# Input projections of a two-layer trunk: norm, turn, modulation and splitting tile by tile with the first panel's products

## The reference, cut to what matters

```
def rms_norm(x, g):
    y = xf * lax.rsqrt(jnp.mean(xf * xf, axis=-1, keepdims=True) + EPS)
    return (y * g.astype(jnp.float32)).astype(x.dtype)
def modulate(x, g, shift, scale):
    return rms_norm(x, g) * (1 + scale) + shift
...
    hp = modulate(xp, norm_mix[l], mp[0], mp[1])
    hs = modulate(xs, norm_mix[l], ms[0], ms[1])
    # even layer: split_even(hp @ even_w_in[j]), split_even(hs @ even_w_in[j])   1024 x 2304
    # odd layer:  split_odd(hp @ odd_w_in[j]),  split_odd(hs @ odd_w_in[j])      1024 x 3616
```

## Time and profile before

| | |
|---|---|
| median of 3 runs | 4213.06 us (4207.27 to 4214.35) |
| profiled execution, its own time | 4200.83 us |
| its span (first to last instruction) | 4199.0 us |
| TensorE busy / weight loads busy | 85% / 64% of the span |
| VectorE, ScalarE, GpSimd busy | 55%, 41%, 14% |
| mean granted TensorE clock | 0.915 of full |
| `project` of layer 0 begins | at 231.08 us (first DMA issue) |
| `project` of layer 1 begins | at 1979.94 us |

### The profile page before, as it was taken

One profiled execution on the slowest core, in us unless ns is written; L12 is line 12 of the kernel. 1 busy time (PEld: TensorE's weight loads), 2 busy tenths in 40 slices (PEclk: granted clock), 3 DMA queues, 4 the chain that ended last, 5 costly groups with the idle time before them and its releaser, 6 DMA issues. The chain is left out here.

```text
span 4199.0 us, 56311 instructions
## 1 busy us (share of the span) xinstructions
PE 3582.2 (85%) x22440; PEld 2694.4 (64%) x22440; DVE 2326.6 (55%) x3515; ACT 1701.2 (41%) x2591; POOL 589.7 (14%) x499
## 2 busy tenths in 40 slices
PE   5969887998769999996899887429996679999995
PEld 1449855665646666664799765429995556666663
DVE  5133333334568788785312453545555667878884
ACT  2031155002346566663211166514434355656553
POOL 0020041221100010000300000025641101000000
PEclk8979998998879999998899998759997889999997
DMA  4132195514448887885442201343325458788885
GB/s 162 67 116 96 63 309 168 159 48 161 173 157 292 301 286 282 292 287 197 117 120 90 109 23 60 111 111 82 99 58 191 156 202 299 273 290 294 299 282 196
DMA packets 378504, 743.15 MB, mean 177 GB/s; under 512 B 99512, under 2 KB 222535, under 8 KB 377080
## 3 DMA queue, kind: packets, MB, share of 16 engines
q1 hardware_dynamic: 358906, 682.76, 46.6%
q0 software_dynamic: 16720, 56.41, 5.5%
q10 hardware_dynamic: 2618, 0.40, 0.1%
HBM read 634.01 MB, written 106.10 MB: 176 GB/s over the span
## 5 line engine op out<-in xcount | busy, mean ns | idle before, releaser
L2425 DVE TENSOR_TENSOR moe_w_low<-ffn_w,moe_w_high 128x1024 fp32r<-128x1024 f32 x768 | 897.7, 1219 | 77.9 <-ACT moe_w_high L2351 75.3
L2351 ACT ACTIVATE moe_w_high<-ffn_w 128x1024 fp32r<-128x1024 f32 x768 | 778.0, 1053 | 219.0 <-DMA ffn_w<-moe_w_gate 127.1
L2275 PE MATMUL moe_small<-ffn_w,ffn_xpT 128*16 128x512 f32 x2048 | 238.3, 594 | 0.0
L2255 PE MATMUL moe_G<-moe_w_high,moe_xT_high 128*128 128x512 f32 x512 | 185.4, 443 | 20.2 <-DVE moe_xT_low L2389 13.3
L224 PE MATMUL proj_mm<-proj_hT_low,proj_w_high 128*128 128x384 f32 x576 | 193.2, 335 | 0.0
L224 PE MATMUL proj_mm<-proj_hT_high,proj_w_low 128*128 128x384 f32 x576 | 193.1, 335 | 0.0
L224 PE MATMUL proj_mm<-proj_hT_high,proj_w_high 128*128 128x384 f32 x576 | 193.1, 335 | 0.0
L2949 PE MATMUL gdnc_a<-gdnc_T,gdnc_kg 128*128 128x64 f32 (+1 forms) x864 | 102.1, 267 | 87.8 <-ACT gdnc_T L2999 85.6
L224 PE MATMUL proj_mm<-proj_w_high,proj_hT_low 128*128 128x416 f32 (+1 forms) x504 | 176.0, 349 | 0.0
L224 PE MATMUL proj_mm<-proj_w_high,proj_hT_high 128*128 128x416 f32 (+1 forms) x504 | 175.5, 348 | 0.0
L224 PE MATMUL proj_mm<-proj_w_low,proj_hT_high 128*128 128x416 f32 (+1 forms) x504 | 174.6, 346 | 0.0
(11 more groups left out here) (479 smaller groups left out, 7437.3 us busy)
## 6 DMA issues: line engine op xcount, KB each, us to landing
ffn_w<-moe_w_gate SPq DMA_DIRECT2D x256, 512.0 KB, 6.4
ffn_w<-moe_w_up SPq DMA_DIRECT2D x256, 512.0 KB, 7.2
ffn_w<-moe_w_down SPq DMA_DIRECT2D x256, 512.0 KB, 5.6
attnrun_m_w<-w_ada SPq DMA_DIRECT2D x40, 1024.0 KB, 11.1
scratch_conv<-proj_zf POOLq DMA_DIRECT2D x24, 512.0 KB, 2.9
scratch_tm<-proj_tm SPq DMA_DIRECT2D x45, 208.0 KB, 2.0
scratch_spec<-front_room SPq DMA_DIRECT2D x36, 256.0 KB, 2.1
proj_w_raw<-even_w_in SPq DMA_DIRECT2D x24, 384.0 KB, 3.8
```

The lines of the kernel that those rows point to most:

```text
L2255: mm = nc.tensor.matmul(bank[:, half, :], stat[a][:, k, :], cut[b][:, half * BANK:(half + 1) * BANK], start=k == 0 and i == 0, stop=k == K ...
L2275: nc.tensor.matmul(out, stat, w, start=k == 0, stop=k == KD - 1, tile_position=(0, 32 * q)).then_inc(small_done, 1)
L2351: nc.scalar.activation(w_high[n % CUT_ROOM][:], raw_rows(wall, n), ACT.Copy).then_inc(w_up, 1)
L2425: nc.vector.tensor_tensor(w_low[n % CUT_ROOM][:], raw_rows(wall, n), w_high[n % CUT_ROOM][:].bitcast(F32), ALU.subtract).then_inc(w_cut, 1)
```

## The change

The shared `Norm` is no longer used here; its steps are written out per token tile, between each other.

- SP loads tile 0 of `x` first and puts the weight pieces between the tiles of `x` (`pieces_with`): piece 0 after tile 0, pieces 1 and 2 after tile 1, piece 3 after tile 2, piece 4 after tile 4, piece 5 after tile 5, pieces 6 and 7 after tile 8. Each piece from 3 on waits for `w_cut` as before.
- ACT takes square, sum and root one tile at a time: tiles 0 to 2, then for every tile t the rounding of tile t (one instruction of 1024 columns), the root of tile t + 3, and the take of the product of tile t - 2. The squares go into the place of the last tile of `hT_low` instead of a tile of their own.
- DVE scales tile t + 1, then modulates tile t in eight instructions of 128 columns. It subtracts tile 0's low part itself, and splits the pieces at fixed tiles: 0 before the first scaling, 1 after it, 2 and 3 with tile 0, and one piece of panel 1 after each of the tiles 2, 4, 6 and 8.
- PE turns tile t + 1 (eight transposes into two banks) before the products of tile t. The products of tile t wait for `hT_cut` of that tile alone; those of tile 0 wait for the pieces one by one.
- POOL subtracts the low parts of tiles 1 to 8, one instruction of 1024 columns each. `hT_raw` is two buffers of a whole tile instead of three of 512 columns.

```
@@ -217,11 +217,11 @@
-def three_passes(nc, out, lhs, rhs, ks):
+def three_passes(nc, out, lhs, rhs, ks, first=True, last=True):
     passes = [(k, a, b) for k in ks for a, b in ((0, 0), (0, 1), (1, 0))]
     for n, (k, a, b) in enumerate(passes):
-        mm = nc.tensor.matmul(out, lhs(a, k), rhs(b, k), start=n == 0, stop=n == len(passes) - 1)
+        mm = nc.tensor.matmul(out, lhs(a, k), rhs(b, k), start=first and n == 0, stop=last and n == len(passes) - 1)
     return mm
@@ -260,7 +260,7 @@
         w_high, w_low = ([s.sb(f"w_{n}{i}", [P, KD, PW], F32R) for i in range(2)] for n in ("high", "low"))
-        hT_raw = [s.sb(f"hT_raw{i}", [P, BANK]) for i in range(3)]
+        hT_raw = [s.sb(f"hT_raw{i}", [P, KD, P]) for i in range(2)]
         w_raw = [s.sb(f"w_raw{i}", [P, KP, PW]) for i in range(3)]
@@ -272,7 +272,13 @@
             bias_in = [s.sem(f"bias_in{h}") for h in range(2)]
-        norm = Norm(s, nc, keep, l, 0, x, None)
+        squares = hT_low[:, :, (NT - 1) * P:]
+        ss = s.sb("ss", [P, NT])
+        rstd = s.sb("rstd", [P, NT])
+        eps = s.sb("eps", [P, 1])
+        turn_bank = [s.ps(f"turn{i}", [P, BANK]) for i in range(2)]
+        eps_set, squared, rooted, recip, scaled, turned, taken = (
+            s.sem(n) for n in ("eps_set", "squared", "rooted", "recip", "scaled", "turned", "taken"))
         banks = [s.ps(f"mm{i}", [P, BANK]) for i in range(6)]
@@ -284,7 +290,6 @@
         blk = s.block()
-        chunks = [(k, at, width, c) for at, width, c in token_groups() for k in range(KD)]
         @blk.sync
@@ -310,18 +315,18 @@
                     sp.dma_start(io["tm"][l][t * P:(t + 1) * P, p * tmw:(p + 1) * tmw], out[n % 4][:]).then_inc(tm_out[n % 4], 16)
-            for m in range(3):
-                piece_in(m)
-            load_x(sp, io, x, x_in, io["x_of"][l])
-            for m in range(3, 2 * PIECES):
-                piece_in(m)
+            pieces_with = {0: (0,), 1: (1, 2), 2: (3,), 4: (4,), 5: (5,), NTS: (6, 7)}
+            for t in range(NT):
+                load_x(sp, io, x, x_in, io["x_of"][l], t)
+                for m in pieces_with.get(t, ()):
+                    piece_in(m)
             for n in range(2, NP + 2):
...
                 if not even and n == 3:
-                    sp.wait_ge(norm.turned, len(chunks))
+                    sp.wait_ge(turned, 2 * NT)
                     sp.wait_ge(pad_out, 16)
@@ -333,10 +338,10 @@
         def _(pool):
-            for n, (k, at, width, _) in enumerate(chunks):
-                pool.wait_ge(hT_up, n + 1)
-                nc.gpsimd.tensor_tensor(hT_low[:, k, at:at + width], hT_raw[n % 3][:, 0:width],
-                                        hT_high[:, k, at:at + width].bitcast(F32), ALU.subtract).then_inc(hT_cut, 1)
+            for t in range(1, NT):
+                pool.wait_ge(hT_up, t + 1)
+                at = slice(t * P, (t + 1) * P)
+                nc.gpsimd.tensor_tensor(hT_low[:, :, at], hT_raw[t % 2][:], hT_high[:, :, at].bitcast(F32), ALU.subtract).then_inc(hT_cut, 1)
             if not even:
@@ -361,10 +366,21 @@
         def _(pe):
-            norm.tensor(pe)
+            def turn(t):
+                pe.wait_ge(scaled, t + 1)
+                for f in range(2):
+                    if t:
+                        pe.wait_ge(taken, 2 * (t - 1) + f + 1)
+                    for j in range(4):
+                        k = 4 * f + j
+                        mm = nc.tensor.transpose(turn_bank[f][:, j * P:(j + 1) * P], x[:, t, k * P:(k + 1) * P], keep.ident[:])
+                    mm.then_inc(turned, 1)
+
+            turn(0)
             n = 0
             for p, (_, width) in enumerate(panels):
-                pe.wait_ge(w_cut, PIECES * (p + 1))
+                if p:
+                    pe.wait_ge(w_cut, PIECES * (p + 1))
                 wp = (w_high[p % 2], w_low[p % 2])
@@ -376,13 +392,18 @@
                         if p == 0:
-                            pe.wait_ge(hT_cut, KD * (i // 4 + 1))
-                        mm = three_passes(nc, banks[n % 6][:, 0:width], lambda a, k: hp[a][:, k, i * P:(i + 1) * P],
-                                          lambda a, k: wp[a][:, k, 0:width], range(KD))
+                            if i + 1 < NT:
+                                turn(i + 1)
+                            pe.wait_ge(hT_cut, i + 1)
+                        for m in range(PIECES):
+                            if p == i == 0:
+                                pe.wait_ge(w_cut, m + 1)
+                            mm = three_passes(nc, banks[n % 6][:, 0:width], lambda a, k: hp[a][:, k, i * P:(i + 1) * P],
+                                              lambda a, k: wp[a][:, k, 0:width], range(m * KP, (m + 1) * KP), m == 0, m == PIECES - 1)
                     else:
...
                         if p == NTM:
-                            pe.wait_ge(hT_cut, 3 * KD)
+                            pe.wait_ge(hT_cut, NT)
                         mm = three_passes(nc, banks[n % 6][:, 0:TG], lambda a, k: wp[a][:, k, j * P:(j + 1) * P],
@@ -390,15 +411,33 @@
         def _(act):
-            norm.scalar(act, lambda eng, t: eng.wait_ge(x_in[t], 16))
-            for n, (k, at, width, _) in enumerate(chunks):
-                act.wait_ge(norm.taken, n + 1)
-                nc.scalar.activation(hT_high[:, k, at:at + width], hT_raw[n % 3][:, 0:width], ACT.Copy).then_inc(hT_up, 1)
-            for n in range(TMN):
+            def root(t):
+                act.wait_ge(x_in[t], 16)
+                if t == 0:
+                    act.wait_ge(eps_set, 1)
+                else:
+                    act.wait_ge(squared, t)
+                nc.scalar.activation(squares, x[:, t, :].rearrange("p (k c) -> p k c", c=P), ACT.Square, accum_out=ss[:, t:t + 1]).then_inc(squared, 1)
+                act.wait_ge(squared, t + 1)
+                nc.scalar.activation(rstd[:, t:t + 1], ss[:, t:t + 1], ACT.Sqrt, bias=eps[:], scale=1.0 / D).then_inc(rooted, 1)
+
+            def take_rows(n):
                 act.wait_ge(mm_done, n + 1)
...
                 nc.scalar.activation(out[n % 4][:], banks[n % 6][:, 0:tmw], ACT.Copy).then_inc(tm_done, 1)
+
+            for t in range(3):
+                root(t)
+            for t in range(NT):
+                act.wait_ge(taken, 2 * t + 2)
+                nc.scalar.activation(hT_high[:, :, t * P:(t + 1) * P], hT_raw[t % 2][:], ACT.Copy).then_inc(hT_up, 1)
+                if t + 3 < NT:
+                    root(t + 3)
+                if t >= 2:
+                    take_rows(t - 2)
+            for n in range(NT - 2, TMN):
+                take_rows(n)
             act.wait_ge(pads, 2)
@@ -442,20 +481,38 @@
                                                ALU.mult, ALU.add).then_inc(zf_done, 1)
-            norm.vector_eps()
-            for m in range(3):
-                piece(m)
-            for g in range(3):
-                norm.vector_scale(dve, g)
-            piece(3)
-            for n, (k, at, width, c) in enumerate(chunks):
-                dve.wait_ge(norm.turned, n + 1)
-                if n >= 3:
-                    dve.wait_ge(hT_cut, n - 2)
-                co = keep.coef[:, l, 0, c]
-                nc.vector.tensor_scalar(hT_raw[n % 3][:, 0:width], norm.banks[n % 2][:, 0:width],
-                                        co[:, 0, k:k + 1], co[:, 1, k:k + 1], ALU.mult, ALU.add).then_inc(norm.taken, 1)
-            panel(1)
+            def scale_rows(t):
+                dve.wait_ge(rooted, t + 1)
+                nc.vector.reciprocal(rstd[:, t:t + 1], rstd[:, t:t + 1]).then_inc(recip, 1)
+                dve.wait_ge(recip, t + 1)
+                nc.vector.tensor_scalar(x[:, t, :], x[:, t, :], rstd[:, t:t + 1], None, ALU.mult).then_inc(scaled, 1)
+
+            def modulate(t):
+                co = keep.coef[:, l, 0, 1 if t == NTS else 0]
+                if t >= 2:
+                    dve.wait_ge(hT_cut, t - 1)
+                for f in range(2):
+                    dve.wait_ge(turned, 2 * t + f + 1)
+                    for k in range(4 * f, 4 * f + 4):
+                        ins = nc.vector.tensor_scalar(hT_raw[t % 2][:, k, :], turn_bank[f][:, (k - 4 * f) * P:(k - 4 * f + 1) * P],
+                                                      co[:, 0, k:k + 1], co[:, 1, k:k + 1], ALU.mult, ALU.add)
+                    ins.then_inc(taken, 1)
+
+            nc.vector.memset(eps[:], EPS).then_inc(eps_set, 1)
+            piece(0)
+            scale_rows(0)
+            piece(1)
+            for t in range(NT):
+                if t + 1 < NT:
+                    scale_rows(t + 1)
+                modulate(t)
+                if t == 0:
+                    piece(2)
+                    dve.wait_ge(hT_up, 1)
+                    nc.vector.tensor_tensor(hT_low[:, :, 0:P], hT_raw[0][:], hT_high[:, :, 0:P].bitcast(F32), ALU.subtract).then_inc(hT_cut, 1)
+                    piece(3)
+                if t in (2, 4, 6, 8):
+                    piece(PIECES + t // 2 - 1)
```

## The result

| | before | changed |
|---|---|---|
| median, first timing | 4210.17 us (4 runs) | 4162.74 us (4160.56 to 4168.26) |
| ratio, first timing | | 0.989, 95% interval 0.9875 to 0.9905 |
| ratio in a second and a third timing | | 0.9903 (0.9886 to 0.992), 0.9897 (0.988 to 0.9913) |
| profiled execution, its own time | 4200.83 us | 4168.26 us |

The change makes the kernel about 1% faster: 47 us in the first timing, 40 and 44 in the others. Equal programs differ by 15 to 20 us from run to run here, and even the begin of the first projection moves from 228 to 233 us, so I read single effects from the traces, in microseconds behind the begin S of the stage, and use the timings for the total.

What follows compares the result with a forecast made beforehand. It took the projection stage as a prologue leaving TensorE nearly useless, then a TensorE-bound body. Shortening the prologue saves 18.0 us in layer 0 and 17.8 in layer 1: 4213 - 36 = 4177 us, own range 4168 to 4188, whole range 4163 to 4199.

Steps and rivals of the forecast that it cites:

- the clock term: First panel of both layers: gaps before the products cost TensorE some granted clock, about 2 us a layer.
- the rival with TensorE's pace: First panel: POOL never late, TensorE's own work sets 5.2 and 5.5 us a tile; 4167 us, chance 0.12.
- First product, S + 15.3: Layer 0's projection prologue: first product starts 15.3 us after the stage's begin instead of 49.5.
- early landing of tile 0: Stage's first load: tile 0 of x lands at S + 3.6; some 5 us later if behind three pieces' time.
- Products of tile 0, 5.4 us: First panel, layer 0: 4.16 us of products plus 1.3 for a slow start, until S + 20.8.
- Pace 5.7 and 5.9: First panel, layers 0 and 1: us per tile from tile 1's products on, set by the slowest loop.
- The loop over two tiles: First panel: modulation's end, rounding, POOL, products, four transposes, next modulation; 10.96 us, 5.5 a tile, longer than other loops.
- the even loop: First panel, tiles 2, 4, 6, 8: a piece's split delays POOL 0.4 us; 11.4 us, 5.7 a tile.
- The covers: Panel 1's pieces, SP's stores, late x tiles, roots, POOL's loads and bias table cost nothing; narrowest cover 7 us.
- DVE behind POOL: First panel: each scaling stands behind POOL's subtraction, 7.1 us a tile; 4195 us, chance 0.20.
- The low clock: First panel: gaps lower TensorE's clock, products 8.3 us, 10.3 a tile; 4253 us, chance 0.03.
- the queue: SP's stores behind piece 8's load, awaiting piece 5's split at S + 38; ACT needs the first after S + 49.

Runs made afterwards that it cites:

- turn inside: Changed kernel with TensorE turning tile t + 2 in the middle of tile t's products, not t + 1 ahead of them: 4157.01 us, 0.9887 to before.
- roots two in front: Changed kernel with ACT taking the root of tile t + 2 instead of t + 3: 4177.46 us, 0.9938 to the kernel before.
- Pieces last: Changed kernel with the second panel's four pieces split behind tile 8, not after tiles 2, 4, 6, 8: 4194.08 us, 0.9975 to before.
- the pieces last and the stores first: Changed kernel, second panel's pieces split behind tile 8, SP's stores of tiles 0 to 6 ahead of loads of pieces 7 and 8: 4163.91 us, 0.9907.
- both, stores first: Changed kernel, turn inside the products, second panel's pieces behind tile 8, SP's stores ahead of loads of pieces 7 and 8: 4154.37 us, 0.9877.
- its repetition: The kernel of 'both, stores first' timed again, beside the changed kernel on one chip: 4160.74 us, 0.9894 to the kernel before.

## Why the prediction was right

The mechanism was right, and the traces show it term by term; the time agrees less well than the terms do.

- **The number.** 4177 us was forecast and 4162.74 measured, 14 us less. That is below the forecast's own 4168 to 4188 and level with the lower end of the whole range, 4163; as a ratio it lies inside (0.989 measured, 4163 / 4213.06 = 0.988). Of the 14 us, 4 are the clock term below, 3 the median before (4213.06 taken, 4210.17 measured beside the change), and 7 are what the first timing, 47 us, had above the traces' 40. By this time alone the rival with TensorE's pace, 4167, would have been the nearer one; only the traces' pace and waits rule it out.
- **First product, S + 15.3.** Measured 15.0 in both layers. The early landing of tile 0 (S + 3.6) is exact: its square began at 236.34, S + 3.55.
- **Products of tile 0, 5.4 us.** Measured 7.0 (247.74 to 254.72). The slow start is 2.8 us and not 1.3: the granted clock was 0.50 until 252.8. It cost nothing: POOL's part of tile 1 came later anyway, at 256.12, with TensorE's products at 256.18, S + 23.4, where I had 23.9.
- **Pace 5.7 and 5.9.** Measured 5.75 and 5.93. The loop over two tiles was named, and "turn inside" shows that it was the cause. One piece of it was misjudged: I had 10.96 for the loop and 0.4 for a piece that holds POOL off. Without any pieces the loop takes 11.25, and a piece costs some 0.15: POOL starts on time, but its subtraction beside the split takes 2.52 to 2.54 us instead of 2.36 to 2.39, which gives the 11.40 measured. The sum of the even loop, 11.4, so came out right by two errors that cancel, a loop 0.3 too short and a piece 0.25 too dear. The 0.3 are the products up to the next turn (4.27, not 4.16), the first four transposes (0.71, not 0.6) and three hand-overs of 0.04 to 0.07, less 0.1 for modulation and rounding.
- **Clock, 2.0 and 2.2 us.** This term was not there. The granted clock was 1.00 from 256 to 301, and also with gaps of 1.3 to 1.5 us before every tile. Without the term the sum was 18.0 + 17.8 + 4.2 = 40.0 us, and the two traces give 40.3. This is the mis-sized term of the forecast.
- **The covers.** Panel 1 started without a gap. One place was closer than I wrote. In layer 1 POOL's bias table (3840 KB), written from 2035.59 and landed by 2067.16, now ran beside the loads and stores of the second panel, and ACT waited 12.3 us for one of the stores, which no take of that panel did before:

```profile
2068.47 1.61 ACT L428 ACTIVATE proj_tm<-proj_mm 128x416 f32<-128x416 f32 x3 [12.30 <-DMA scratch_tm<-proj_tm]
```

  Three takes were late, and six banks hid them: TensorE was busy for 42.00 of 42 us from 2038 on. I had looked only at who wants the table, and not at what its transfer runs beside. The store wanted was issued only at 2054.27, behind four loads that took SP 15.8 us where they took 6.1 before. In every other run of the new panel ACT has such a wait too, 7.4 to 12.6 us long, and it ends within 3.3 us of the table's landing. That it is this table is argued from these times; no run moved it.
- **The rivals.** DVE behind POOL did not set the pace: three scalings a layer stand behind POOL, as written, beside the products. The run with the roots two in front shows that the rival stands one tile of lookahead away. TensorE's own pace is 5.05 a tile, less than the 5.2 that I gave it, as eight transposes among products cost 0.9. The low clock and the queue did not occur in the changed kernel. "Pieces last" shows what the queue would have cost.

## What to carry to other kernels

When a prologue is cut into tiles and laid over the products, the pace is rarely that of one engine: add up the chain from a tile's hand-over back to the buffer or bank that the next tile but one needs, and see which long piece of work stands in that chain only because of the order in which it is written. Here the 4 us of products stood in it, and writing the next turn into their middle took them out. Before small steps are moved to the end, follow every queue that waits for them: a store behind a load behind a split can stop an engine that has nothing to do with any of them.

## What the runs showed of the hardware

- A scaling of 1024 columns on DVE (one SBUF input, 0.75 us alone) that is issued while POOL subtracts takes 1.38 to 1.64 us with the roots two in front and 2.69 to 2.70 us, three times a layer, in the changed kernel; it ends half a microsecond behind POOL. The rounding of a weight piece does the same (2.72 to 2.93 us instead of 0.55 to 0.59, once a layer with the pieces last and the stores first). Modulations from PSUM (2.64 us for eight) keep their time beside POOL's 2.4 us subtraction, in every kernel.
- TensorE kept its full clock through a panel with an idle gap of 0.3 to 1.5 us before each tile (1.00 granted). Twice it did not behind a longer gap: 1.80 us before 254.19 in 'both, stores first', shown here, and 1.89 us before 2025.42 in its repetition. No run varied the gap alone. After a gap of 14.27 us the first product took 0.69 us again, as one does at the lower level, where 0.33 is usual.

```profile
256.00:258.00 2.00, 2.00 (x9) 1.90 (x8) 0.00 (x0) 1.52 (x4) 2.00 (x1) 0.50 0.00 0
```

- Transposes alone can run at the full clock: in the kernel before, from 263 to 269, TensorE did nothing else, was busy for 3.14 of the 6 us, and had 1.00 granted; before (257 to 263) and after (269 to 275) it was 0.56 and 0.79.
